# HGRN recurrence: finest level from raw keys, eight mask groups in two PSUM banks, coarse blocks copied by ScalarE, no state work in the last tile

## The chip, the cores and the metric

The kernel runs on one core of a Trainium2 chip. The metric is the device time of one launch in microseconds. Engines are TensorE (PE, with its weight loads PEld), VectorE (DVE), ScalarE (ACT), GpSimd (POOL) and SyncE (SP, here the queue of the weight loads).

## The reference, cut

Two blocks over 512 tokens of width 1024. The first has a gated linear attention (GLA) in chunks of 64 tokens, a short convolution and a window attention; the second runs twice (two layers) and has an indexed attention and the HGRN recurrence. Its intra-chunk part has a decay for each pair of positions and each key channel:

```python
def step(S, xs):
    qc, kc, vc, bc = xs                      # bc = cumsum(log_f) in the chunk
    inter = jnp.einsum('bhtd,bhde->bhte', qc * jnp.exp(bc), S)
    diff = bc[:, :, :, None, :] - bc[:, :, None, :, :]
    decay = jnp.exp(jnp.where(causal[:, :, None], diff, -jnp.inf))
    A = jnp.einsum('bhtd,bhsd,bhtsd->bhts', qc, kc, decay)
    intra = jnp.einsum('bhts,bhse->bhte', A, vc)
    b_last = bc[:, :, -1:, :]
    S = jnp.exp(b_last[:, :, 0, :])[..., None] * S + jnp.einsum(
        'bhsd,bhse->bhde', kc * jnp.exp(b_last - bc), vc)
    return S, inter + intra
```

S after the last chunk is not an output.

## The kernel before, in words

Everything is float32. Projections are products of high and low halves (three matmuls of 512 columns each for one pair of tiles): ScalarE makes the high half of a weight panel (L1029), GpSimd the low half (L1599), SyncE loads panels into a ring of three. Each engine's program is written by hand in its own order and engines meet by semaphores.

The HGRN recurrence (`core`, on TensorE, ScalarE and VectorE) works on tiles of 128 tokens and two heads at a time: eight units per layer, numbered 0 to 7 here, unit u being tile m = u // 2 and heads 2(u % 2), 2(u % 2) + 1. It runs in two layers, from about 983 to 1162 us and from about 1837 to 2015 us of the span. In a unit:

- TensorE sums the logs of the decays with 9 mask groups of 128 columns (7 levels, the running sum, the rest to the tile's end): for each head three banks of 384 columns, L614 and L615. ScalarE takes the exponent of each head's sums (L1171) into `dec`.
- VectorE copies the tile's decay (L1718), then multiplies: rest x keys (L1722), running sum x queries (L1724), and for each of the 7 levels l the odd blocks of width 128 >> (l+1) by queries and the even ones by keys (L1730, 14 operations).
- TensorE turns the rest-keys (L627), computes the diagonal scores (L631) and the scores of the levels (L635, each waits for its `lev_ready`). ScalarE copies the turned keys to `kdt` (L1177). VectorE puts the diagonal (L1734) and the seven levels (L1744) into `attT` by predicated copies from PSUM.
- TensorE makes the unit's output from `attT` and the state (L647, L649), and the state's addend from `kdt` (L653). VectorE copies the output (L1749) and updates the state (L1757).

Between these parts each engine takes steps of other work (`take_on(side, ...)`): projections of the attention's queries, keys and values, 12 matmuls a step. The steps are fixed: one between the sums of the two heads, two after them, one after the levels, one after the output. In units 2 to 5 ScalarE's share of the two steps after the sums is the root of a normalisation: L1212, L1215, L1220, L1222 of 1024 elements each with two table loads (in unit 2 the rectified keys, L1458, too). VectorE's share of the side work is the rotary embedding (L2121, L2127, L2130, L1822, L1824, L2136), the scores of the index (L2047 to L2052) and the selection of the largest (L2059, L2061).

The GLA core (`core_chunked`, from about 108 to 238 us) has the same eight units with two levels and one bank per head.

## Time and profile before

| | |
|---|---|
| time, median of 3 runs | 2625.77 us (2624.51 to 2629.67) |
| profiled execution: span | 2626.2 us |
| its mean granted TensorE clock | 0.994 |
| TensorE busy | 2553.7 us, 97% of the span |
| VectorE busy | 1149.1 us, 44% |
| ScalarE busy | 991.7 us, 38% |
| GpSimd busy | 1082.5 us, 41% |
| chain that ended last | TensorE 80%, VectorE 14%, ScalarE 4%, DMA 1% |

The profiled execution's span is 0.4 us above the median of the three timed runs, so sums made in the trace can be set against the median as they are. A busy share of TensorE counts a matmul from its issue to its modelled end; those ends overlap the next one's start, so prices of matmuls are taken from the distance between starts.

### The profile page before, as it was taken

Reading aid. Unit: us, or ns where it says so; the run is one execution under the profiler, and the core shown is the slowest. Engines: PE = TensorE matmul, PEld = TensorE weight load, DVE = VectorE, ACT = ScalarE, POOL = GpSimd, SP = SyncE. Lnnn points to the kernel's source line nnn. Section 1 sums busy time; section 2 is a strip of 40 time slices with the busy share of each in tenths; the row PEclk is TensorE's granted clock in tenths of the full one; section 3 lists DMA queues with packets and bytes.
Section 4 is the critical chain, followed back from the end, with each engine's and each line's share of the span. In section 5 each row is a group of like instructions: output and inputs, shape, how many; then the busy total and the mean of one; then the engine's idle time right before and its main releaser. Section 6 shows DMA issues by size and latency. Waiting matters only on the chain.

```text
span 2626.2 us, 30117 instructions
## 1 busy us (share of the span) xinstructions
PE 2553.7 (97%) x12440; PEld 2088.4 (80%) x12440; DVE 1149.1 (44%) x1977; ACT 991.7 (38%) x1128; POOL 1082.5 (41%) x816
## 2 busy tenths in 40 slices
PE   7999999999999999989999999999999999999998
PEld 5887777878888787877788888888787778888887
DVE  6452353365424366987434111124698743411112
ACT  4523543343323454635434222235463543422220
POOL 4333334544545443213264444444321326444442
PEclk9999999999999999999999999999999999999999
DMA  4222222322333232222132222233222212222222
GB/s 160 80 79 66 82 80 81 96 97 82 98 99 98 90 97 69 73 64 66 49 96 96 97 96 96 97 97 97 69 73 65 65 50 95 97 97 96 96 96 80
DMA packets 209012, 226.81 MB, mean 86 GB/s; under 512 B 4482, under 2 KB 198236, under 8 KB 208748
## 3 DMA queue, kind: packets, MB, share of 16 engines
q1 hardware_dynamic: 208368, 224.74, 27.0%
q8 instruction: 98, 1.61, 0.3%
q14 instruction: 39, 0.31, 0.0%
q10 hardware_dynamic: 507, 0.15, 0.0%
HBM read 217.01 MB, written 2.10 MB: 83 GB/s over the span
## 4 chain that ended last, share of the span: by engine, by line
PE 80%; DVE 14%; ACT 4%; DMA 1%; issue 1%; SPq 0%; POOL 0%; DVEq 0%; ACTq 0%
PE psum L487 71%; PE psum L764 1%; PE psum L776 1%; PE psum L753 1%; DVE top L2059 1%; DVE attT L1744 1%; ACT wh L1029 1%; DVE ul L1935 1%; PE psum L635 1%; DVE score L2061 1%; DVE dec L1730 1%; DVE normed L1686 1%; DVE merged L1958 1%; DVE tmp L1822 1%; DVE tmp L1824 0%
## 5 line engine op out<-in xcount | busy, mean ns | idle before, releaser
L1599 POOL TENSOR_TENSOR wl<-raw,wh 128x512 fp32r<-128x512 f32 x812 | 1082.3, 1367 | 1519.0 <-ACT wh L1029 1387.3
L487 PE MATMUL psum<-uh,wh 128*128 128x512 f32 x2016 | 803.5, 399 | 13.1 <-DVE ul L1935 4.3
L487 PE MATMUL psum<-uh,wl 128*128 128x512 f32 x2016 | 789.5, 392 | 0.0
L487 PE MATMUL psum<-ul,wh 128*128 128x512 f32 x2016 | 789.0, 391 | 0.0
L1029 ACT CAST wh<-raw 128x2048 fp32r<-128x2048 f32 (+1 forms) x206 | 387.0, 1880 | 299.2 <-DMA raw<-in_w_ffn_out 120.0
L487 PEld LDWEIGHTS psum<-uh,wh 128*128 128x128 f32 x2016 | 380.9, 189 | 101.0 <-issue 13.7
L487 PEld LDWEIGHTS psum<-uh,wl 128*128 128x128 f32 x2016 | 380.5, 189 | 80.7
L487 PEld LDWEIGHTS psum<-ul,wh 128*128 128x128 f32 x2016 | 381.2, 189 | 77.9 <-issue 2.4
L487 PE MATMUL psum<-fh,wl 128*128 128x512 f32 x528 | 205.7, 390 | 0.0
L487 PE MATMUL psum<-fl,wh 128*128 128x512 f32 x528 | 205.7, 390 | 0.0
L487 PE MATMUL psum<-fh,wh 128*128 128x512 f32 x528 | 205.7, 390 | 0.0
L1981 DVE TENSOR_TENSOR xT<-xT,psum 128x1024 f32<-128x1024 f32 (+1 forms) x48 | 56.0, 1166 | 293.0 <-PE psum L487 292.8
L2027 DVE TENSOR_TENSOR tmp<-tmp,psum 128x1024 f32<-128x1024 f32 x22 | 26.9, 1221 | 358.6 <-PE psum L487 358.5
L487 PEld LDWEIGHTS psum<-fl,wh 128*128 128x128 f32 x528 | 99.2, 188 | 20.6
L487 PEld LDWEIGHTS psum<-fh,wl 128*128 128x128 f32 x528 | 99.2, 188 | 20.5
L487 PEld LDWEIGHTS psum<-fh,wh 128*128 128x128 f32 x528 | 99.2, 188 | 20.4
L487 PE MATMUL psum<-vh,wh 128*128 128x512 f32 x280 | 111.4, 398 | 3.0 <-ACT gk L1546 1.4
L487 PE MATMUL psum<-vh,wl 128*128 128x512 f32 x280 | 109.2, 390 | 0.0
L487 PE MATMUL psum<-vl,wh 128*128 128x512 f32 x256 | 99.8, 390 | 0.0
L1389 ACT ACTIVATE tmp<-psum 128x1024 f32<-128x1024 f32 x22 | 22.6, 1029 | 178.5 <-PE psum L487 175.3
L487 PE MATMUL psum<-brh,wh 128*128 128x512 f32 x224 | 89.4, 399 | 0.0
L1171 ACT ACTIVATE dec<-psum 128x1152 f32<-128x1152 f32 x32 | 36.3, 1135 | 139.4 <-PE psum L615 139.4
(353 smaller groups left out, 3343.1 us busy)
## 6 DMA issues: line engine op xcount, KB each, us to landing
raw<-in_w_in SPq DMA_DIRECT2D x78, 1024.0 KB, 5.3
raw<-in_w_ffn_in SPq DMA_DIRECT2D x44, 1024.0 KB, 5.1
raw<-in_w_up SPq DMA_DIRECT2D x22, 1024.0 KB, 5.1
raw<-in_w_ffn_out SPq DMA_DIRECT2D x16, 1024.0 KB, 5.1
raw<-in_w_down SPq DMA_DIRECT2D x8, 1024.0 KB, 5.1
raw<-in_w_out SPq DMA_DIRECT2D x8, 1024.0 KB, 5.1
raw<-in_w_ffn_out SPq DMA_DIRECT2D x8, 768.0 KB, 4.4
raw<-in_w_o SPq DMA_DIRECT2D x4, 1024.0 KB, 5.2
```

What stands on the lines that cost most here:

```text
L487: ins = mm(dst, x, y, start=first and i == 0, stop=last and i == len(todo) - 1)
L635: ins = mm(level_scores(l)[:, i, :, :], dec[:, i, l, :], odd_blocks(dec[:, i, l, :], l), start=True, stop=True)
L753: ins = mm(X[e][:, 0:(b1 - b0) * P], q[HD * e:HD * (e + 1), p, m * P:(m + 1) * P], kof(2 * p + e)[:, b0 * P:b1 * P], start=True, stop=True)
L764: ins = nc.tensor.transpose(X[2][:, c * P:(c + 1) * P], prob[i % 2][:, e, b * P:(b + 1) * P], ident)
L776: ins = mm(X[3][HD * e:HD * (e + 1), 0:P], vof(2 * p + e, b), probT[i % 2][:, e, (b - b0) * P:(b - b0 + 1) * P], start=(b == b0), stop=(b ...
L1029: nc.scalar.copy(wh[p % 3][:, 0:nk * width], raw[p % 3][:, 0:nk * width]).then_inc(S.hi_done, 1)
L1171: fn(dec[:, i, :, :].rearrange("p (b l) t -> p b (l t)", b=3), X4[:, 1:4, 0:3 * P], ACT.Exp).then_inc(S.dec_done, 1)
L1599: ins = nc.gpsimd.tensor_tensor(wl[p % 3][:, w], raw[p % 3][:, w], wh[p % 3][:, w].bitcast(F32), ALU.subtract)
L1686: v.scalar_tensor_tensor(normed[:, c % 2, :], xT[:, c, :], g(c), scale[:], ALU.mult, ALU.mult).then_inc(S.n_normed, 1)
L1730: ins = v.tensor_tensor(e[:, :, :, part, :], e[:, :, :, part, :], x[:, :, :, part, :], ALU.mult)
L1981: v.tensor_tensor(x, x, src, ALU.add).then_inc(pair_free[(n.q - 1) % 2], 1)
L2027: v.tensor_tensor(tmp[2][:], tmp[0][:], src, ALU.mult).then_inc(pair_free[(n.q - 1) % 2], 1)
```

## The change

Three things, in the HGRN core, and the third in the GLA core too.

1. The finest level (blocks of one position) needs no decay on its keys and one step of decay on its queries. It gets no mask group any more: ScalarE takes the exponent of the odd positions' logs out of `lg` into a new tile `last`, VectorE multiplies `last` by the odd queries, and TensorE uses `gk` as it is. Eight mask groups stay, in two banks of 512 columns. The levels' scores move to other columns (l + 2), and the state's addend from X[1] to the second half of X[3]; TensorE waits for the state before a unit's output and not before its sums.
2. The two coarsest levels' blocks are copied from PSUM to `attT` by ScalarE, in three copies behind its `kdt` copy, without a mask. VectorE waits for them (`blocks_done`) before its first predicated copy, and has five levels left.
3. In the last tile (units 6 and 7) nothing is done for the next state: no turned keys, no `kdt`, no addend, no update, no decay copy (none in the first tile either), and no running sum x queries in the first tile.

```diff
 # TensorE, core
-                    if u > 0:
-                        pe.wait_ge(S.state_done, t.up(S.state_done))
...
-                        for b in range(3):
-                            cols = slice(3 * P * b, 3 * P * (b + 1))
-                            mm(X[1 + b][:, 0:3 * P], lth[:, u % 2, i, :], summask[:, cols], start=True, stop=False)
-                            ins = mm(X[1 + b][:, 0:3 * P], ltl[:, u % 2, i, :], summask[:, cols], start=False, stop=True)
+                        for b in range(2):
+                            cols = slice(4 * P * b, 4 * P * (b + 1))
+                            mm(X[1 + b], lth[:, u % 2, i, :], summask[:, cols], start=True, stop=False)
+                            ins = mm(X[1 + b], ltl[:, u % 2, i, :], summask[:, cols], start=False, stop=True)
...
+                            if l + 1 < LEVELS:
+                                keys, queries = dec[:, i, l, :], odd_blocks(dec[:, i, l, :], l)
+                            else:
+                                keys, queries = gk[:, 2 * hp + i, tok], last[:, i, :]
...
+                    if m + 1 < NT:
+                        pe.wait_ge(S.kdt_done, t.up(S.kdt_done))
+                    if 0 < u < CORE_UNITS - 1:
+                        pe.wait_ge(S.state_done, t.up(S.state_done))
 # ScalarE, core
+                        if i == 0:
+                            odd = lg[:, 2 * hp:2 * hp + 2, m * P:(m + 1) * P].rearrange("p h (g two) -> p h g two", two=2)
+                            fn(last[:], odd[:, :, :, 1], ACT.Exp)
...
                     take_on(side, core_steps(total, u, 1))
+                    if m + 1 < NT:
+                        act.wait_ge(S.kd_T, t.up(S.kd_T))
+                        nc.scalar.copy(kdt[:], X[0][:, 0:2 * P].rearrange("p (h f) -> p h f", h=2)).then_inc(S.kdt_done, 1)
+                    act.wait_ge(S.att_done, t.up(S.att_done))
+                    t.up(S.att_done, len(LEVEL_ENDS) - 1)
+                    half, quarter = P // 2, P // 4
+                    nc.scalar.copy(attT[0:half, :, half:P], level_scores(0)[0:half, :, 0, :])
+                    for g in range(2):
+                        keys = slice(half * g, half * g + quarter)
+                        ins = nc.scalar.copy(attT[keys, :, half * g + quarter:half * (g + 1)], level_scores(1)[keys, :, g, :])
+                    ins.then_inc(S.blocks_done, 1)
 # VectorE, core
                     dve.wait_ge(S.att_done, t.up(S.att_done))
+                    dve.wait_ge(S.blocks_done, t.up(S.blocks_done))
...
-                    for l in range(LEVELS):
+                    for l in range(2, LEVELS):
...
 # the levels after which TensorE signals att_done
-LEVEL_ENDS = (1, 3, 6)
+LEVEL_ENDS = (1, 5, 6)
 # the end of core_chunked on TensorE
                 pe.wait_ge(S.out_read, t.up(S.out_read))
-                pe.wait_ge(S.state_done, t.up(S.state_done))
                 finish(side)
```

ScalarE's program in unit 2 of a layer. Before, from the root of the side work to the next unit:

```order
L1222 ACTIVATE tmp<-tmp 128x1024 [waits act_chain]
L1458 ACTIVATE keys_72<-psum 128x1024 [waits pair_full]
L1177 COPY kdt<-psum 128x256 [waits kd_T]
L1029 CAST wh<-raw 128x2048 [waits raw_in1]
L1171 ACTIVATE dec<-psum 128x1152 [waits sums_done]
```

And now:

```order
L1248 ACTIVATE tmp<-tmp 128x1024 [waits act_chain]
L1484 ACTIVATE keys_73<-psum 128x1024 [waits pair_full]
L1193 COPY kdt<-psum 128x256 [waits kd_T]
L1197 COPY attT<-psum 64x2x64 [waits att_done]
L1200 COPY attT<-psum 32x2x32 x2
L1040 CAST wh<-raw 128x2048 [waits raw_in1]
L1185 ACTIVATE last<-lg 128x128 [waits sums_done]
```

The three copies stand behind everything that ScalarE did before `kdt`, and ahead of the next panel's high half. VectorE's program at the same place, before:

```order
L1744 COPY_PREDICATED attT<-pairmask,psum 128x2x64 [waits dve_chain]
L1744 COPY_PREDICATED attT<-pairmask,psum 128x4x32 [waits dve_chain]
L1744 COPY_PREDICATED attT<-pairmask,psum 128x8x16 [waits att_done,dve_chain]
L1744 COPY_PREDICATED attT<-pairmask,psum 128x16x8 [waits dve_chain]
L1744 COPY_PREDICATED attT<-pairmask,psum 128x32x4 [waits att_done,dve_chain]
```

And now, with the sine of the rotary embedding ahead of it:

```order
L2160 SCALAR_TENSOR_TENSOR tmp<-tmp,small,sinT 128x1024 [waits turned]
L1768 COPY_PREDICATED attT<-pairmask,psum 128x256 [waits blocks_done,att_done,dve_chain]
L1778 COPY_PREDICATED attT<-pairmask,psum 128x8x16 [waits att_done,dve_chain]
L1778 COPY_PREDICATED attT<-pairmask,psum 128x16x8 [waits dve_chain]
L1778 COPY_PREDICATED attT<-pairmask,psum 128x32x4 [waits dve_chain]
```

The two coarse copies are gone from VectorE, and its first one waits for ScalarE. On TensorE, at the start of unit 7, before:

```order
L627 MATMUL psum<-const,dec 128x128 [waits out_read,kd_ready,dec_done]
L627 MATMUL psum<-const,dec 128x128
L631 MATMUL psum<-gq,gk 128x128 x2
L635 MATMUL psum<-dec 128x64 [waits lev_ready]
L635 MATMUL psum<-dec 128x64
```

And now:

```order
L633 MATMUL psum<-gq,gk 128x128 [waits out_read,dec_done]
L633 MATMUL psum<-gq,gk 128x128
L641 MATMUL psum<-dec 128x64 [waits lev_ready]
L641 MATMUL psum<-dec 128x64
```

The turned keys are gone there, and with them the wait for VectorE's L1722.

## Rows read from the trace of the kernel before

**Rows 1.** The page: busy time of the engines.
```profile
PE 2553.7 (97%) x12440; PEld 2088.4 (80%) x12440; DVE 1149.1 (44%) x1977; ACT 991.7 (38%) x1128; POOL 1082.5 (41%) x816
```

**Rows 2.** Timeline of TensorE, one head's sums and what follows: start, us.
```profile
1026.35 0.34 PE L614 MATMUL psum<-summask,lth 128*128 128x384 f32 x1
...
1027.41 0.39 PE L487 MATMUL psum<-uh,wh 128*128 128x512 f32 x1
1027.64 0.40 PE L487 MATMUL psum<-ul,wh 128*128 128x512 f32 x1
```

**Rows 3.** Timeline of TensorE, HGRN cores: its idle time in brackets.
```profile
1021.01 1.14 PE L647 MATMUL psum<-attT,gv 128*128 128x128 f32 x4 [1.89 <-DVE attT L1744]
...
1049.02 0.41 PE L614 MATMUL psum<-summask,lth 128*128 128x384 f32 x1 [0.66 <-DVE state L1757]
...
1060.31 0.41 PE L627 MATMUL psum<-const,dec 128*128 128x128 f32 x2 [1.31 <-DVE dec L1722]
...
1067.71 0.49 PE L647 MATMUL psum<-attT,gv 128*128 128x128 f32 x2 [0.61 <-DVE attT L1744]
...
1110.24 0.49 PE L647 MATMUL psum<-attT,gv 128*128 128x128 f32 x2 [0.48 <-DVE attT L1744]
...
1136.28 0.80 PE L647 MATMUL psum<-attT,gv 128*128 128x128 f32 x2 [4.53 <-DVE attT L1744]
...
1153.90 0.41 PE L627 MATMUL psum<-const,dec 128*128 128x128 f32 x2 [0.73 <-issue]
...
1179.32 1.13 PE L806 MATMUL psum<-ik,iq 64*128 64x512 f32 x4 [0.78 <-ACT silu L1227]
...
1913.67 0.41 PE L627 MATMUL psum<-const,dec 128*128 128x128 f32 x2 [1.33 <-DVE dec L1722]
```

**Rows 4.** Windows: busy us of PE, PEld, DVE, ACT, POOL, then granted clock.
```profile
1020.00:1025.00 5.00, 3.99 (x15) 3.52 (x16) 3.20 (x7) 0.00 (x0) 5.00 (x5) 0.66 0.00 0
1910.00:1915.00 5.00, 3.67 (x23) 2.95 (x22) 4.76 (x20) 4.94 (x5) 0.00 (x0) 1.00 0.68 184
```

**Rows 5.** Timeline of ScalarE, units 2, 4 and 5 of the first layer.
```profile
1041.26 0.36 ACT L1177 COPY kdt<-psum 128x256 f32<-128x256 f32 x1
...
1085.90 0.35 ACT L1177 COPY kdt<-psum 128x256 f32<-128x256 f32 x1
...
1106.41 0.35 ACT L1177 COPY kdt<-psum 128x256 f32<-128x256 f32 x1
```

**Rows 6.** Timeline of VectorE, units 2 to 5.
```profile
1039.74 0.45 DVE L1734 COPY_PREDICATED attT<-pairmask,psum 128x256 f32<-128x256 uint8 x1
1040.22 2.63 DVE L1744 COPY_PREDICATED attT<-pairmask,psum 128x128 f32<-128x128 uint8 x7
...
1043.28 3.32 DVE L2049 SCALAR_TENSOR_TENSOR score<-keys,iw,score 128x256 f32<-128x256 f32 x3
...
1085.04 0.45 DVE L1734 COPY_PREDICATED attT<-pairmask,psum 128x256 f32<-128x256 uint8 x1
...
1107.10 0.45 DVE L1734 COPY_PREDICATED attT<-pairmask,psum 128x256 f32<-128x256 uint8 x1
```

**Rows 7.** Timeline of GpSimd, the panel made beside unit 2's side work.
```profile
1043.51 5.52 POOL L1599 TENSOR_TENSOR wl<-raw,wh 128x512 fp32r<-128x512 f32 x4 [16.21 <-ACT wh L1029]
```

**Rows 8.** Timeline of TensorE, then VectorE, the last unit of the GLA core.
```profile
227.66 0.38 PE L692 MATMUL psum<-const,cdec 128*128 128x128 f32 x2
227.88 1.06 PE L697 MATMUL psum<-cdec 128*128 128x128 f32 x8
...
235.15 0.61 PE L713 MATMUL psum<-gv,kdt 128*128 128x128 f32 x4
235.59 0.60 PE L864 MATMUL psum<-const,tmp 128*128 128x128 f32 x4
...
238.39 0.47 PE L487 MATMUL psum<-uh,wh 128*128 128x512 f32 x1 [2.20 <-DVE state L1813]
...
237.69 0.59 DVE L1813 SCALAR_TENSOR_TENSOR state<-state,small,psum 128x128 f32<-128x128 f32 x2
```

More of the change, by code:

```diff
@@ L344, in build_program @@
         csum = at("csum", 38, [P, 4 * P], F32R)
+        last = at("last", 40, [P, 2, P // 2])
         lth = at("lth", 41, [P, 2, 2, P], F32R)
@@ L622, in core @@
                     pe.wait_ge(S.dec_done, t.up(S.dec_done))
-                    pe.wait_ge(S.kd_ready, t.up(S.kd_ready))
                     if u + 1 == CORE_UNITS:
                         pe.wait_ge(S.out_read, t.up(S.out_read))
-                    for i in range(2):
-                        ins = nc.tensor.transpose(X[0][:, i * P:(i + 1) * P], dec[:, i, LEVELS + 1, :], ident)
-                    ins.then_inc(S.kd_T, 1)
+                    if m + 1 < NT:
+                        pe.wait_ge(S.kd_ready, t.up(S.kd_ready))
+                        for i in range(2):
+                            ins = nc.tensor.transpose(X[0][:, i * P:(i + 1) * P], dec[:, i, REST, :], ident)
+                        ins.then_inc(S.kd_T, 1)
                     for i in range(2):
@@ L634, in core @@
                         for i in range(2):
[L635 to L636 removed]
+                            if l + 1 < LEVELS:
+                                keys, queries = dec[:, i, l, :], odd_blocks(dec[:, i, l, :], l)
+                            else:
+                                keys, queries = gk[:, 2 * hp + i, tok], last[:, i, :]
+                            ins = mm(level_scores(l)[:, i, :, :], keys, queries, start=True, stop=True)
                         if l in LEVEL_ENDS:
@@ L648, in core @@
                         if m > 0:
-                            ins = mm(X[0][:, i * P:(i + 1) * P], state[:, h, :], dec[:, i, LEVELS, :], start=False, stop=True)
+                            ins = mm(X[0][:, i * P:(i + 1) * P], state[:, h, :], dec[:, i, CUM, :], start=False, stop=True)
                     ins.then_inc(S.out_done, 1)
-                    for i in range(2):
-                        h = 2 * hp + i
-                        ins = mm(X[1][:, i * P:(i + 1) * P], kdt[:, i, :], gv[:, m, h * P:(h + 1) * P], start=True, stop=True)
-                    ins.then_inc(S.kv_done, 1)
+                    if m + 1 < NT:
+                        for i in range(2):
+                            h = 2 * hp + i
+                            ins = mm(X[3][:, (2 + i) * P:(3 + i) * P], kdt[:, i, :], gv[:, m, h * P:(h + 1) * P],
+                                     start=True, stop=True)
+                        ins.then_inc(S.kv_done, 1)
                     take_on(side, core_steps(total, u, 4))
                 pe.wait_ge(S.out_read, t.up(S.out_read))
-                pe.wait_ge(S.state_done, t.up(S.state_done))
                 finish(side)
@@ L710, in core_chunked @@
                     ins.then_inc(S.out_done, 1)
-                    for i in range(2):
-                        h = 2 * hp + i
-                        ins = mm(X[1][:, i * P:(i + 1) * P], kdt[:, i, :], gv[:, m, h * P:(h + 1) * P], start=True, stop=True)
-                    ins.then_inc(S.kv_done, 1)
+                    if m + 1 < NT:
+                        for i in range(2):
+                            h = 2 * hp + i
+                            ins = mm(X[1][:, i * P:(i + 1) * P], kdt[:, i, :], gv[:, m, h * P:(h + 1) * P], start=True, stop=True)
+                        ins.then_inc(S.kv_done, 1)
                     take_on(side, core_steps(total, u, 4))
                 pe.wait_ge(S.out_read, t.up(S.out_read))
-                pe.wait_ge(S.state_done, t.up(S.state_done))
                 finish(side)
@@ L1727, in core @@
                         form = lambda x: x.rearrange("p h (g two w) -> p h g two w", two=2, w=w)
-                        e, q, k = form(dec[:, :, l, :]), form(gq[:, heads, tok]), form(gk[:, heads, tok])
-                        for part, x in ((1, q), (0, k)):
-                            ins = v.tensor_tensor(e[:, :, :, part, :], e[:, :, :, part, :], x[:, :, :, part, :], ALU.mult)
+                        q, k = form(gq[:, heads, tok]), form(gk[:, heads, tok])
+                        if l + 1 < LEVELS:
+                            e = form(dec[:, :, l, :])
+                            for part, x in ((1, q), (0, k)):
+                                ins = v.tensor_tensor(e[:, :, :, part, :], e[:, :, :, part, :], x[:, :, :, part, :], ALU.mult)
+                        else:
+                            ins = v.tensor_tensor(last[:], last[:], q[:, :, :, 1, 0], ALU.mult)
                         ins.then_inc(S.lev_ready, 1)
@@ L1794, in core_chunked @@
                     scaled(C_KEY, gk).then_inc(S.lev_ready, 1)
-                    scaled(C_CUM, gq)
+                    if m > 0:
+                        scaled(C_CUM, gq)
                     take_on(side, core_steps(total, u, 1))
@@ L2413, in shape_constants @@
         start = (t // w) * w
-        sums.append(np.where(odd, (j >= start) & (j <= t), (j > t) & (j < start + w)))
+        if l + 1 < LEVELS:
+            sums.append(np.where(odd, (j >= start) & (j <= t), (j > t) & (j < start + w)))
         pairs.append(((j // w) % 2 == 0) & (t // w == j // w + 1))
```

104 lines of the change are left out of this document (57 added, 47 removed).

## The prediction

> **What bounds the kernel now.** I read the page first: TensorE is busy 97% of the span [rows 1], so the time falls by what TensorE's own program loses, and by those waits of TensorE that really shrink. Work taken off VectorE or ScalarE counts only there. Next I read TensorE's timeline through the HGRN cores for its idle time. Nearly all of it is VectorE's: L647 waits for the last predicated copy in units 1, 3, 5 and 6, L627 for VectorE's L1722 in units 3 and 7, L614 once for the state [rows 3]. The second layer's core shows the same pattern, so I work out one layer and double it. Then the windows: after the 1.89 us wait the granted clock of a 5 us stretch is 0.66, so it stood at the 1.2 GHz level for two thirds of the stretch and at 2.4 GHz for the rest, and TensorE loses (1 - 0.66) x 5 = 1.7 us; after a wait of 1.33 us (1913.67) the stretch stays at 1.00 [rows 3, 4]. So a wait that grows past something between 1.33 and 1.89 us costs 1.7 us more, and one that shrinks below gives 1.7 back. Last I set the timelines of ScalarE and VectorE beside each other, because the change makes VectorE's first predicated copy wait for ScalarE. In unit 2 VectorE starts it at 1039.74, and ScalarE's kdt copy starts only at 1041.26; in unit 4 it is 1085.04 against 1085.90, in unit 5 1107.10 against 1106.41 [rows 5, 6].
>
> **The change's prices.**
>
> Sums: six matmuls of 384 columns take 1.06 us from start to start, one of 512 takes 0.23, four 0.91: 0.15 saved a head, 0.3 a unit [rows 2]. Matmuls on raw keys in place of scaled ones have the same shapes: nothing.
>
> VectorE: seven predicated copies take 2.63 us [rows 6]; the two that go are of the shorter ones, 0.7 with their gaps. The finest level's second multiplication is 0.2, L1722 and L1724 0.34 each where they go, the decay copy 0.2.
>
> ScalarE: its three copies have 128, 64 and 64 elements a partition, together what one kdt copy has. By elements they cost one kdt copy, 0.36 us; if each costs a whole one, 1.08 [rows 5]. They overlap at their ends as others do; I take 0.4 from kdt's end, near the low end because no element is added, and keep 0.25 to 1.1. By the Trainium skill (ScalarE: Activation LUTs, What ACT_TABLE_LOAD costs: an activation with immediate operands takes 186 ns and 0.833 ns an element, neighbours overlap by 93 ns) the estimate would be 0.5 us behind kdt, which would take some 0.5 us off the gain. The exponent of `last` (128 elements) adds about 0.15 a unit and the smaller `dec` exponents take 0.1 off each.
>
> **One layer, unit by unit** (shift of TensorE, measured from the place where it last waited for nobody or was itself waited for).
>
> Unit 0: sums 0.3, less what the extra exponent adds: -0.25.
> Unit 1: L647 waits on a chain that begins with a DMA of the embedding's halves; its start moves by one head's sums, 0.15, and VectorE saves 0.7: -0.85. TensorE itself arrives 0.3 earlier, so the 1.89 us wait becomes about 1.35, by the row of 1.33 just short of a clock drop.
> Unit 2, head: -0.15.
> Units 2 to 3: the first place where the change hurts. ScalarE is at 1041.5 with its kdt copy (0.1 earlier than before) and at 1041.9 with the blocks, so VectorE starts 2.2 us later than 1039.74, saves 0.7, and is 1.5 us later behind it. It had no slack there: from here to L1722 of unit 3 it never idles. Its three score operations take 3.32 us beside GpSimd's panel of 1043.51 [rows 6, 7], twice their price alone; starting later it meets one more of the panel's pieces, 0 to 0.95 more, I take 0.5. So L1722 of unit 3 is 2.0 later, at 1062.2. TensorE comes there earlier: +0.3 from unit 2's output, -0.66 for the state wait of 1049.02, -0.3 for sums, so its 1.31 us wait becomes 3.9 us and, by rows 3 and 4, the clock falls: 1.8 more. From L627 to L647 is 6.8 us of work (1060.31 to 1067.71 less the 0.61 wait [rows 3]): L647 at 1062.2 + 6.8 + 1.8 = 1070.8 in place of 1067.71: +3.1.
> Unit 4: ScalarE 0.25 earlier, blocks at 1086.4 in place of VectorE's 1085.04; the copies end at 1088.8, TensorE arrives at 1087.9: +0.7.
> Unit 5: blocks and VectorE both at 1106.9; the 0.48 us wait goes: -0.5.
> Unit 6: VectorE alone decides (4.53 us wait): decay 0.2, L1722 0.34, level 0.2, copies 0.7: -1.4. The wait stays above 3 us and the clock drops as before.
> Units 6 to 7: from L647 of unit 6 VectorE loses its state update, 1.0 with the wait ahead of it, the decay copy and L1722, and TensorE loses `kdt`'s turns, L653 and 0.3 of sums; TensorE's 0.73 us wait at 1153.90 moves to the first level, 1.75 earlier: -1.75.
> Tail: the 0.78 us wait of 1179.32 hangs on VectorE's chain behind unit 7's output, from which the 0.6 us state update goes: -0.6.
> Sum: -0.25 - 0.85 - 0.15 + 3.1 + 0.7 - 0.5 - 1.4 - 1.75 - 0.6 = -1.7 a layer, -3.4 for two. Unit 1's clock is worth 1.7 a layer if kept; as my 1.35 lies at the row of 1.33 but with an error of some tenths, I count half: -1.7 for two.
>
> GLA core: unit 6 loses two turns (227.66 to 227.88, 0.22) and L653's like L713 (235.15 to 235.59, 0.45); unit 7 loses 0.2, and at its end TensorE, which waited 2.20 us for the state, now waits for the output's copy only, 0.59 less [rows 8]: -1.45. The wait stays about 2.1, so the clock still drops there.
>
> Sum: -3.4 - 1.7 - 1.45 = -6.5 us; from the median 2625.8, 2619.3.
>
> **Rivals.**
>
> The full gain, 2608 us. ScalarE's copies hold nobody up; then units 2 to 3 give 1.5 and unit 4 0.3, a layer -7.3, in all -14.5 - 1.45 - 1.7 = -17.6. It would need ScalarE to reach its kdt copy before VectorE reaches L1734 in unit 2, 1.5 us earlier than the row shows, and nothing in its program ahead of that place goes. Chance 0.13.
>
> Slower, above 2631 us. The mechanism is the wait for ScalarE's blocks, in units 2 and 4 and, beyond 0.4 us, unit 5. Each us that the three copies take costs 1.0 + 1.0 + 0.6 a layer, 5.2 in two. It cancels the gain at 0.4 + 6.5 / 5.2 = 1.65 us and gives a measurable loss at 2.7 us, 0.9 a copy against 0.36 for kdt. With copies at 1.1 us, one more collision with GpSimd and unit 1 at low clock it is still 2626. The Trainium skill has a rule against this part of the change (ScalarE: Activation LUTs, Rules for kernel authors: plain elementwise work belongs on VectorE, which is faster an element); the time here hangs on when ScalarE is free and not on its speed. Chance 0.12.
>
> My forecast, a gain that ScalarE's lateness eats to a large part, 0.75. Its own range: unit 3 without a clock drop takes 1.9 off each layer and both clocks kept 1.7 in all, 2613; copies at 1.1 us, the collision and no clock kept, 2625.
>
> **Chances and range.** A measurement can tell some 0.2%, 5.2 us, from no change: the bound for faster is 2620.5, just above my number. Of the forecast's 0.75 I give 0.42 to faster, 0.30 to same, 0.03 to slower; with the rivals 0.55, 0.31, 0.14. The range 2609 to 2627 leaves out half of the full gain and nearly all of the slower case.
>
> **What the profile after would show.** Right: four matmuls of 512 columns a head; in unit 2 the first predicated copy starts about 2 us later against ScalarE's chain, released by ScalarE's block copies; TensorE's wait before L627's like in unit 3 near 3.9 us and a clock below 1 behind it; a new wait of about 0.9 us in unit 4; unit 6's wait near 3.4; none for the state before the sums; the unit 1 wait at 1.35. Wrong: no VectorE wait on ScalarE in unit 2, or a unit 3 wait below 2 us (then nearer 2610), or blocks that take over 1 us (then no gain). The number hangs most on unit 3, where VectorE's lateness, GpSimd's panel and the clock multiply each other.

## The result, and the profile after

The changed kernel takes 2630.45 us (median of 20 runs, 2627.35 to 2636.07), the kernel before beside it 2626.76 us (20 runs). The ratio is 1.0017, with a 95% interval of 1.0011 to 1.0022: slower by 4 us. That is less than the 0.2% that I had called measurable, but the interval leaves out 1. I had predicted 2619.3 us, 2609 to 2627.

The profiled execution of the changed kernel spans 2629.6 us (before: 2626.2), so it shows the difference. First the page's row of busy times, the answer to [rows 1]:

```profile
PE 2552.7 (97%) x12340; PEld 2080.0 (79%) x12340; DVE 1128.0 (43%) x1893; ACT 1000.6 (38%) x1186; POOL 1084.4 (41%) x816
```

TensorE has 100 matmuls less and is busy 1.0 us less, VectorE is busy 21 us less: the work did go away. What grew is one stretch of TensorE's program. The timeline of TensorE through the first HGRN core, answering to [rows 3] (the same units in the same order; L655 is L647 of before, L629 is L627):

```profile
1016.35 0.71 PE L655 MATMUL psum<-attT,gv 128*128 128x128 f32 x4 [1.96 <-DVE attT L1778]
...
1039.91 0.49 PE L655 MATMUL psum<-attT,gv 128*128 128x128 f32 x2 [0.38 <-DVE attT L1778]
...
1057.77 0.41 PE L629 MATMUL psum<-const,dec 128*128 128x128 f32 x2 [3.88 <-DVE dec L1750]
...
1058.47 5.17 PE L641 MATMUL psum<-dec 128*128 128x64 f32 x24
1063.43 1.05 PE L641 MATMUL psum<-last,gk 128*128 128x64 f32 x4
...
1069.23 0.38 PE L655 MATMUL psum<-attT,gv 128*128 128x128 f32 x2
...
1090.62 0.49 PE L655 MATMUL psum<-attT,gv 128*128 128x128 f32 x2 [1.02 <-DVE attT L1778]
...
1112.17 0.49 PE L655 MATMUL psum<-attT,gv 128*128 128x128 f32 x2 [0.26 <-DVE attT L1778]
...
1137.51 0.80 PE L655 MATMUL psum<-attT,gv 128*128 128x128 f32 x2 [4.38 <-DVE attT L1778]
```

From one unit's output matmul to the next this gives, after against before:

| stretch, first HGRN layer | before us | after us | difference | predicted |
|---|---|---|---|---|
| unit 0 to 1 | 21.42 | 21.28 | -0.14 | -0.85 |
| unit 1 to 2 | 23.11 | 23.56 | +0.45 | -0.15 |
| unit 2 to 3 | 23.59 | 29.32 | +5.73 | +3.1 |
| unit 3 to 4 | 20.48 | 21.39 | +0.91 | +0.7 |
| unit 4 to 5 | 22.05 | 21.55 | -0.50 | -0.5 |
| unit 5 to 6 | 26.04 | 25.34 | -0.70 | -1.4 |
| unit 6 to 7 | 24.32 | 22.68 | -1.64 | -1.75 |

The second layer has +5.70 in the third row and the others within 0.2 of these, except the last (-0.99). The third row is the result: everything else together is a gain, 1.6 us in the first layer and 1.1 in the second.

In that row two things add. The wait ahead of the turned keys is 3.88 us, as predicted. And behind it TensorE is slow. These are the windows (busy us of PE, PEld, DVE, ACT, POOL, then the granted clock, the DMA share and GB/s) over the wait and what follows:

```profile
1055.00:1060.00 5.00, 2.23 (x14) 2.26 (x15) 4.83 (x21) 4.92 (x6) 0.00 (x0) 0.86 0.02 3
1060.00:1065.00 5.00, 5.00 (x24) 4.90 (x24) 3.40 (x9) 2.46 (x4) 2.17 (x2) 0.50 0.00 0
1065.00:1070.00 5.00, 5.00 (x19) 4.05 (x18) 0.63 (x2) 0.00 (x0) 2.80 (x3) 0.61 0.00 0
```

The granted clock is 0.50 in a whole stretch, the 1.2 GHz level, and it is back at 2.4 GHz only at 1068.7. Summed as (1 - clock) x 5, as the prediction did, that is 0.7 + 2.5 + 1.95 = 5.15 us of clock, where I had put 1.8. TensorE needs 11.46 us from L629 to L655; the same stretch before was 6.8 us of work. At 1063.74 VectorE even waits 1.47 us for TensorE's level matmuls, which it did not in this unit before.

VectorE in unit 2, the answer to [rows 6], and ScalarE and GpSimd beside it, the answer to [rows 5, 7]:

```profile
1037.45 0.46 DVE L1768 COPY_PREDICATED attT<-pairmask,psum 128x256 f32<-128x256 uint8 x1 [2.80 <-ACT attT L1200]
1037.94 1.92 DVE L1778 COPY_PREDICATED attT<-pairmask,psum 128x128 f32<-128x128 uint8 x5
1039.90 0.85 DVE L2086 TENSOR_SCALAR score<-keys,iw 128x256 f32<-128x256 f32 x1
1040.79 4.25 DVE L2088 SCALAR_TENSOR_TENSOR score<-keys,iw,score 128x256 f32<-128x256 f32 x3
1045.07 0.29 DVE L2091 TENSOR_TENSOR score<-score,const 128x128 f32<-128x128 f32 x1
1045.40 0.42 DVE L1783 COPY gq<-psum 128x256 f32<-128x256 f32 x1
...
1057.21 0.42 DVE L1750 TENSOR_TENSOR dec<-dec,gk 128x256 f32<-128x256 f32 x1
```

```profile
1036.50 0.36 ACT L1193 COPY kdt<-psum 128x256 f32<-128x256 f32 x1
1036.75 0.26 ACT L1197 COPY attT<-psum 64x128 f32<-64x128 f32 x1
1036.91 0.41 ACT L1200 COPY attT<-psum 32x64 f32<-32x64 f32 x2
...
1039.33 5.42 POOL L1625 TENSOR_TENSOR wl<-raw,wh 128x512 fp32r<-128x512 f32 x4 [17.24 <-ACT wh L1040]
```

VectorE's first predicated copy waits 2.80 us for ScalarE's blocks, whose three copies end 0.46 us behind the `kdt` copy (1036.86 to 1037.32). The prediction had both, with 2.2 for the wait and 0.4 for the copies.

Where the wait of 3.88 us comes from can be read off, with two rows of before that answer to these. They are VectorE's read of the output (L1749, which is L1783 after) and TensorE's first output matmul of unit 2:

```profile
1047.93 0.42 DVE L1749 COPY gq<-psum 128x256 f32<-128x256 f32 x1
```

```profile
1044.12 0.38 PE L647 MATMUL psum<-attT,gv 128*128 128x128 f32 x2
```

From L1749 to L1722 of unit 3 VectorE took 11.82 us before (TensorE's L627 follows it at 1060.31 [rows 3]), and 11.81 after (1045.40 to 1057.21): it never idles there, so all that matters is when it starts. Before, the last predicated copy of unit 2 ended at 1042.85 [rows 6], 5.08 us ahead of L1749 and 1.27 us ahead of L647. After, it ended at 1039.86, 5.54 us ahead of L1783 and 0.05 ahead of L655. TensorE's own work from L647 to L627 was 14.22 us without its waits, and is 13.98. So VectorE is later against TensorE by 1.22 (it used to be done before TensorE came), 0.46 (more of its score operations beside GpSimd) and 0.24 (TensorE's shorter sums), 1.92 in all. Before, TensorE had waited 0.66 + 1.31 = 1.97 us in two places [rows 3]; after, it waits 1.97 + 1.92 = 3.89 us in one, since the wait for the state no longer stands ahead of the sums.

### The profile page after: what moved, and what is told of

Its sections match the earlier page's. It is cut to its first block, busy times and chain, and to the rows that moved or that the text cites. A ratio compares the mean times of both kernels' runs of the same rounds, so it can differ in the third digit from the quotient of the medians.

```text
span 2629.6 us, 29863 instructions
## 1 busy us (share of the span) xinstructions
PE 2552.7 (97%) x12340; PEld 2080.0 (79%) x12340; DVE 1128.0 (43%) x1893; ACT 1000.6 (38%) x1186; POOL 1084.4 (41%) x816
## 4 chain that ended last, share of the span: by engine, by line
PE 79%; DVE 13%; ACT 6%; issue 1%; DMA 1%; SPq 0%; POOL 0%; DVEq 0%; ACTq 0%
PE psum L490 71%; DVE top L2098 1%; PE psum L775 1%; PE psum L787 1%; PE psum L764 1%; PE psum L641 1%; ACT wh L1040 1%; DVE ul L1974 1%; DVE tmp L2100 1%; DVE attT L1778 1%; DVE score L2100 1%; DVE merged L1997 1%; DVE score L2088 0%; PE psum L895 0%; DVE normed L1712 0%
## 5 line engine op out<-in xcount | busy, mean ns | idle before, releaser
L490 PE MATMUL psum<-brh,wl 128*128 128x512 f32 x224 | 87.4, 390 | 0.0
```

What stands on the lines that cost most here:

```text
L490: ins = mm(dst, x, y, start=first and i == 0, stop=last and i == len(todo) - 1)
```

## The experiments

Each was timed against the kernel before on the same chip (6 to 11 runs each), with ratios and 95% intervals. The median of the kernel before was 2625.9 to 2626.4 us there and 2626.8 beside the change, so a difference between two experiments is good to about a microsecond at best. "Pause" is an idle time of TensorE, in unit 3 where nothing else is said.

**1. VectorE copies all levels.** The rest of the change stays.

```
-                    nc.scalar.copy(attT[0:half, :, half:P], level_scores(0)[0:half, :, 0, :])
...
-                    dve.wait_ge(S.blocks_done, t.up(S.blocks_done))
...
-                    for l in range(2, LEVELS):
+                    for l in range(LEVELS):
```

> The changed kernel with its second part undone: VectorE copies all seven levels, ScalarE none. Theory A (ScalarE's blocks come late in unit 2, VectorE and then TensorE wait, and TensorE's clock falls behind a 3.9 us wait and stays low through the small level matmuls): the wait ahead of unit 3's turned keys goes back to about 1.3 us, the clock stays at 1.00 there, and the time is about 2616 us, some 11 below the kernel before. Rival B (the loss is in the other parts: the extra exponent, the matmuls on raw keys, the state's addend in another bank): the clock or the waits of unit 3 hardly change and the time stays at 2628 or above.

Measured: 2628.52 us, 1.0013 (1.0005 to 1.0022). ScalarE's lateness is then not the whole reason: without any wait for ScalarE the kernel is still slower than before. It is 1.9 us below the change, which these runs don't tell apart. TensorE's timeline and the windows:

```profile
1058.84 0.41 PE L629 MATMUL psum<-const,dec 128*128 128x128 f32 x2 [3.60 <-DVE dec L1743]
```

```profile
1055.00:1060.00 5.00, 1.40 (x10) 1.19 (x8) 4.76 (x19) 4.93 (x5) 0.00 (x0) 0.92 0.21 47
1060.00:1065.00 5.00, 5.00 (x26) 5.00 (x25) 3.89 (x13) 2.86 (x3) 2.07 (x2) 0.50 0.02 3
1065.00:1070.00 5.00, 5.00 (x16) 4.12 (x16) 1.79 (x5) 0.00 (x0) 2.90 (x3) 0.56 0.00 0
```

The pause is 3.60 us and the clock falls as far. VectorE's three score operations take 4.41 us here (3.32 before, where the first of them, begun ahead of GpSimd's panel, takes 0.48 and the two beside it 1.38 each): they fall on another part of the panel, and the collision puts back 1.09 of what ScalarE's absence gives. The removed wait and the shorter sums are in this kernel too.

**2. ScalarE copies only where it is early**, in units 0, 1, 6 and 7; VectorE copies all levels in units 2 to 5.

```
+                    if u in (0, 1, 6, 7):
+                        act.wait_ge(S.att_done, first)
+                        nc.scalar.copy(attT[0:half, :, half:P], level_scores(0)[0:half, :, 0, :])
...
+                    for l in range(2 if u in (0, 1, 6, 7) else 0, LEVELS):
```

> The changed kernel, ScalarE copying the two coarse levels' blocks only in units 0, 1, 6 and 7, where it is free before VectorE comes; VectorE copies them in units 2 to 5. Theory A: as with all copies on VectorE and another 0.7 us a layer in unit 6: about 2614.5 us. Rival B: 2628 or above.

Measured: 2624.87 us, 0.9995 (0.9986 to 1.0004): no difference from the kernel before that can be told, where a gain of some 12 us was expected. The reason is the same: the pause in unit 3 is 3.62 us, and 3.45 us of clock are lost from 1055 to 1065. But it is 5.6 us less than the change and 3.7 less than experiment 1, and the intervals don't meet. ScalarE's copies cost time in units 2 to 5, where they are late, and save time in the other units.

**3. ScalarE's blocks alone**, on the kernel before.

```
+                    nc.scalar.copy(attT[0:half, :, half:P], level_scores(0)[0:half, :, 0, :])
...
+                    dve.wait_ge(S.blocks_done, t.up(S.blocks_done))
...
-                    for l in range(LEVELS):
+                    for l in range(2, LEVELS):
```

> The kernel before with the change's second part alone: ScalarE copies the two coarse levels' blocks in every unit, nothing else. Theory A: units 3 and 4 of each layer lose some 6 us together, the other units gain at most 1: about 2636 us, and the clock is low for some 10 us in unit 3. Rival B: no slower than before, 2620 to 2627.

Measured: 2629.88 us, 1.0016 (1.0007 to 1.0025). A loss of 3.6 us, but far from the 2636 expected. TensorE's waits in units 2 and 3 of the first layer:

```profile
1039.64 0.49 PE L648 MATMUL psum<-attT,gv 128*128 128x128 f32 x2 [0.35 <-DVE attT L1755]
1046.19 0.42 PE L615 MATMUL psum<-summask,lth 128*128 128x384 f32 x1 [2.19 <-DVE state L1768]
1057.48 0.41 PE L628 MATMUL psum<-const,dec 128*128 128x128 f32 x2 [1.30 <-DVE dec L1732]
```

Together 3.49 us, nearly as long as in the changed kernel, but in two pieces, and the windows from 1055 to 1070 show a clock of 1. So the blocks' lateness costs time with the clock up, too. (In the second layer the clock does fall behind the 2.17 us pause, for 1.7 us.) This row gave me the next theory: the pieces matter, not only the sum.

**4. The pause filled.** The changed kernel, with work that nobody reads in unit 3: it adds 16 matmuls of 512 columns. The wait ahead of them keeps the bank that they write free; in the trace of the change that state is done at 1046.34, long ahead of it, so it holds nobody up.

```
+                    if u == 3:
+                        pe.wait_ge(S.state_done, t.at["state_done"] + 1)
+                        for _ in range(16):
+                            mm(X[3], uh[:, 0, 0:P], uh[:, 0, :], start=True, stop=True)
                     pe.wait_ge(S.dec_done, t.up(S.dec_done))
```

> The changed kernel with 16 extra matmuls of 512 columns on idle columns of PSUM in unit 3 of each layer, ahead of the wait for VectorE's turned keys; they take 3.65 us at full clock, a little less than the 3.88 us wait, and do nothing for the result. Theory A: the wait shrinks to about 0.2, nothing comes later for it, the clock stays at 1.00 and each layer gains the 4.7 us that the work behind the wait took too long: about 2621 us. Rival C (the slow stretch behind the wait is not the clock's but the levels' own, held by VectorE's multiplications): no change against the changed kernel, 2630.

Measured: 2621.92 us, 0.9987 (0.9978 to 0.9996). More work, 8.5 us less time. The same three windows:

```profile
1055.00:1060.00 5.00, 4.75 (x34) 4.08 (x33) 4.86 (x21) 4.93 (x8) 0.00 (x0) 1.00 0.01 3
1060.00:1065.00 5.00, 5.00 (x34) 4.44 (x34) 3.56 (x8) 1.91 (x1) 2.99 (x3) 1.00 0.00 0
1065.00:1070.00 5.00, 5.00 (x26) 4.12 (x25) 4.78 (x6) 0.79 (x2) 2.04 (x2) 1.00 0.01 2
```

So the clock in unit 3 is what makes the change a loss. Of the 10.3 us of clock in two layers 8.5 come back.

**5. The wait split again.** Nothing added, one wait moved back to where the kernel before had it.

```
                     pe.wait_ge(S.lt_lo, t.up(S.lt_lo))
+                    if 0 < u < CORE_UNITS - 1:
+                        pe.wait_ge(S.state_done, t.up(S.state_done))
...
-                    if 0 < u < CORE_UNITS - 1:
-                        pe.wait_ge(S.state_done, t.up(S.state_done))
                     for i in range(2):
```

> The kernel after, with one line moved: in the HGRN core TensorE waits for the state's update ahead of the decay sums, as the kernel before did, and no longer ahead of the output matmuls. No work is added or taken away. In the trace of the kernel after, the update in unit 3 of layer 1 ends at 1046.34, and TensorE's sums began at 1044.11 and its wait for the turned keys was 3.88 us: so now about 2.3 us of waiting stand ahead of the sums and 1.6 ahead of the turned keys, 3.9 together as in the kernel after. Theory S (the change joined two waits into one, and the long one lets the clock fall): the granted clock from 1055 to 1070 stays near 1, as in the experiment that filled the wait (2621.9), and the time is 2620 to 2624. Theory T (the sum of waiting decides, however it is split): 2629 to 2632, clock low over the same 11 us or already at the sums.

Measured: 2621.75 us, 0.9985 (0.9976 to 0.9994), 8.7 us less than the change. (One of its 11 runs took 3628.12 us, the others 2620.33 to 2626.66; I have no cause for it.) TensorE's timeline:

```profile
1044.29 0.47 PE L617 MATMUL psum<-summask,lth 128*128 128x512 f32 x1 [2.20 <-DVE state L1792]
...
1063.26 0.49 PE L655 MATMUL psum<-attT,gv 128*128 128x128 f32 x2 [0.87 <-DVE attT L1778]
```

and the windows behind the wait and in unit 3:

```profile
1040.00:1045.00 5.00, 2.80 (x13) 2.00 (x12) 4.83 (x7) 0.00 (x0) 2.56 (x2) 0.97 0.00 0
1045.00:1050.00 5.00, 5.00 (x17) 3.98 (x16) 4.86 (x5) 1.53 (x3) 0.00 (x0) 0.69 0.00 0
...
1055.00:1060.00 5.00, 5.00 (x41) 4.60 (x40) 4.60 (x17) 4.93 (x6) 0.00 (x0) 1.00 0.27 61
1060.00:1065.00 5.00, 4.13 (x25) 3.31 (x24) 2.72 (x8) 2.55 (x5) 2.33 (x2) 1.00 0.00 0
```

The expectation of two pauses was not quite right, and the difference is instructive. The first pause does let the clock fall, by 0.15 + 1.55 = 1.7 us, but these 1.7 us lie ahead of the place where TensorE would have waited 1.6 us more for VectorE. That second pause is gone, so this clock loss is free. A slow stretch costs where TensorE is behind, and nothing where it would wait anyway.

**6. The same, with VectorE copying all levels** (experiment 1 with the wait moved back).

> The same move of the wait in the kernel in which VectorE copies all seven levels (2628.5, its wait in unit 3 3.60 and 3.66 us): parts 1 and 3 of the change, but without the late wait and without ScalarE's blocks. Theory S: the wait splits into about 2.3 and 1.3, no low clock in units 3, and some 3 us a layer less: 2621 to 2624; with the experiment above it says what ScalarE's copies are worth when the clock is out of it. Theory T: 2628 to 2630, as with the late wait.

Measured: 2621.23 us, 0.9983 (0.9974 to 0.9992), 7.3 us less than with the late wait. Against experiment 5 ScalarE's copies make 0.5 us, nothing that can be told. That is a balance and not a price of nothing, as the next experiment shows.

**7. The same, with ScalarE's blocks in units 0, 1, 6 and 7** (experiment 2 with the wait moved back).

> The same move of the wait in the kernel in which ScalarE copies the blocks in units 0, 1, 6 and 7 alone (2624.9, its wait in unit 3 3.62 us with a low clock from 1055 to 1065). Theory S: 2617 to 2620, better than every kernel so far. Theory T: 2624 to 2626.

Measured: 2618.42 us, 0.9974 (0.9962 to 0.9985), 6.5 us less than with the late wait. In all three forms the one moved wait is worth 6 to 9 us. This kernel is also 2.8 us below experiment 6 and 3.3 below experiment 5: with the wait in its place, too, block copies are worth having where ScalarE is early and cost about as much where it is late. (The three intervals overlap, so these two figures are rough.) This trace also holds the same pause twice with two outcomes. Timeline of TensorE and windows, first layer, then second:

```profile
1057.36 0.41 PE L631 MATMUL psum<-const,dec 128*128 128x128 f32 x2 [1.46 <-DVE dec L1752]
1058.06 4.32 PE L643 MATMUL psum<-dec 128*128 128x64 f32 x24
...
1908.34 0.41 PE L631 MATMUL psum<-const,dec 128*128 128x128 f32 x2 [1.45 <-DVE dec L1752]
1909.03 2.85 PE L643 MATMUL psum<-dec 128*128 128x64 f32 x24
```

```profile
1060.00:1065.00 5.00, 5.00 (x21) 4.61 (x21) 4.22 (x10) 2.18 (x3) 2.74 (x3) 0.50 0.00 0
...
1910.00:1915.00 5.00, 5.00 (x33) 4.29 (x32) 4.75 (x14) 3.14 (x4) 1.75 (x2) 1.00 0.00 0
```

A pause of 1.46 us cost 3.4 us of clock, one of 1.45 us in the same place of the other layer none.

**8. The same, with the pauses of units 1 and 6 filled** by work that nobody reads.

```
+                    for _ in range({1: 8, 6: 16}.get(u, 0)):
+                        mm(X[0][:, 0:P], gk[:, 2 * hp, tok], gq[:, 2 * hp, tok], start=True, stop=True)
                     pe.wait_ge(S.pairs_done, t.up(S.pairs_done))
```

> The kernel of the experiment above, and in each HGRN core TensorE also computes 8 matmuls in unit 1 and 16 in unit 6 whose results nobody reads (gk by gq, 128 columns, 0.22 us each, into the first quarter of the bank of the output), ahead of its waits of 1.96 us and 4.4 us for the score blocks. They fill 1.8 and 3.5 us of waiting and none of them is needed. If the clock is what these waits cost beside themselves, the lows at 1015 to 1020, 1130 to 1140, 1905 to 1910 and 1980 to 1990 (granted 0.66, 0.75, 0.91, 0.73, 0.74, 0.91 in that kernel) go, about 1.7 + 1.7 us a layer: 2612 to 2615. If work behind these waits is anyway bound by VectorE, TensorE only waits longer at the next place: 2617 to 2620.

Measured: 2618.16 us, 0.9971 (0.9961 to 0.9981): no gain over experiment 7, although the low clock of unit 6 did go (unit 1 had none left in the trace of experiment 7; the granted clocks in the expectation are those of experiment 2). The edit also takes the wait for `kdt` ahead of the fill. In unit 7 TensorE's wait for VectorE's levels grew from nothing to 1.09 us in the first layer and 1.07 in the second: the second of the two outcomes I had named. Behind unit 6 VectorE sets the time, and TensorE's clock is free there.

**9. Wide work ahead of the narrow.** The changed kernel with its 3.88 us pause; in unit 3 the 12 projection matmuls come directly behind it, ahead of the turns and the level matmuls.

```
                         pe.wait_ge(S.kd_ready, t.up(S.kd_ready))
+                        if u == 3:
+                            take_on(side, core_steps(total, u, 2))
+                            take_on(side, core_steps(total, u, 3))
```

> The kernel after, with the state's wait where it put it; in unit 3 of each HGRN core TensorE takes its 12 matmuls of 512 columns of projection work, which stand behind the level matmuls, right behind its wait for the turned keys instead, ahead of the two turns and of the 28 level matmuls of 64 columns. No work is added and the pause itself (3.88 us) stays. In the kernel after, 6.8 us of work behind that pause took 11.5 us at a granted clock of 0.50 to 0.61. Theory U (what follows the pause decides: behind wide matmuls the clock comes back sooner, behind the narrow level matmuls it stays low): the low stretch costs 1.7 to 3.4 us in place of 5.1, and 2625 to 2628. Theory V (the length of the pause decides, whatever follows): the low stretch costs the same 5.1, now partly under wide matmuls, the level scores come 3 to 5 us later and nothing hides VectorE's copies: 2633 to 2637.

Measured: 2630.44 us, 1.0017 (1.0008 to 1.0026), the time of the changed kernel. TensorE's timeline and the windows:

```profile
1059.03 0.77 PE L490 MATMUL psum<-uh,wh 128*128 128x512 f32 x1 [3.86 <-DVE dec L1754]
...
1063.94 2.79 PE L644 MATMUL psum<-dec 128*128 128x64 f32 x24
...
1068.80 0.75 PE L659 MATMUL psum<-attT,gv 128*128 128x128 f32 x2 [1.62 <-DVE attT L1782]
```

```profile
1060.00:1065.00 5.00, 5.00 (x27) 4.28 (x26) 3.05 (x11) 1.39 (x3) 0.00 (x0) 0.80 0.01 3
1065.00:1070.00 5.00, 3.38 (x26) 3.25 (x26) 2.21 (x6) 2.44 (x4) 2.44 (x2) 0.89 0.00 0
1070.00:1075.00 5.00, 5.00 (x22) 4.34 (x22) 3.60 (x6) 0.00 (x0) 2.51 (x3) 0.77 0.00 2
```

About the clock theory U holds: behind the same pause the low stretch now costs 0.7 + 1.0 = 1.7 us (the window ahead of these, 1055 to 1060, is at 0.86 as in the changed kernel), and the level matmuls run at full speed, 2.79 us in place of 5.17. About the time neither theory holds: nothing covers VectorE's copies any more, so there is a new pause of 1.62 us, and behind it the clock falls again for 1.7 us. What the order of the work saves in one place it gives back in the next.

**10. No state work in the last tile, alone**, on the kernel before.

```
+                    if m + 1 < NT:
+                        pe.wait_ge(S.kd_ready, t.up(S.kd_ready))
+                        for i in range(2):
+                            ins = nc.tensor.transpose(X[0][:, i * P:(i + 1) * P], dec[:, i, LEVELS + 1, :], ident)
```

(and so for `kdt`, L653, the decay and the state, in both recurrences)

> The kernel before with part 3 of the change alone: no state work in the last tile of either recurrence (units 6 and 7), everything else as before (nine mask groups, keys times decay in the finest level, VectorE copies all seven levels, the state's wait ahead of the sums). By the prediction's rows it takes from TensorE two turns (0.41) and four matmuls (0.61) in each of two units of three cores, of which the 4.53 us wait of unit 6 swallows one unit's, and 0.9 to 2.2 us of VectorE's tail at the end of the GLA core: 2622 to 2625. If GLA's end is bound by the transfer or by the output's read, 2625 to 2626.

Measured: 2621.71 us, 0.9979 (0.9970 to 0.9988). This part alone is worth 4.2 us, 0.3 us beyond the good end of the 2622 to 2625 expected. Part 1 (two banks of sums, raw keys) was not run alone; experiment 6 is part 1 and part 3 with the wait in its old place, and differs from this by 0.5 us, so part 1 is worth nothing that can be told. The parts don't simply add: part 2 alone cost 3.6 us, on top of parts 1 and 3 (experiment 5 against 6) 0.5.

**11. Half of the fill** of experiment 4, 8 matmuls.

> The kernel after with 8 matmuls of 512 columns ahead of the wait for the turned keys in unit 3 in place of 16 (1.85 us of unneeded work in a pause of 3.88, so some 2.0 us of pause stay). With 16 the low clock went and the time was 2621.9, with none it is 2630.5. If the clock falls by the length of the one pause, 2.0 us here leave it up (a pause of 2.20 before the sums cost 1.55 us of clock in the split kernel, one of 2.19 none): 2621 to 2624. If any pause ahead of the narrow level matmuls lets it fall (1.46 us did, at 1057.36 in the split kernel with early blocks): 2625 to 2628, a loss of 3.4 us a layer less what later slack takes up.

Measured: 2624.72 us, 1.0000 (0.9990 to 1.0011), between the two answers, and the trace suggests why. The pause is 2.05 us in the first layer and 2.08 in the second:

```profile
1055.00:1060.00 5.00, 3.77 (x19) 3.80 (x19) 4.93 (x19) 4.00 (x8) 0.00 (x0) 0.62 0.01 3
1060.00:1065.00 5.00, 5.00 (x21) 4.71 (x22) 2.48 (x7) 1.88 (x1) 3.05 (x3) 0.50 0.00 0
...
1910.00:1915.00 5.00, 2.92 (x22) 2.41 (x20) 4.79 (x19) 4.93 (x5) 0.00 (x0) 1.00 0.02 3
1915.00:1920.00 5.00, 5.00 (x34) 4.44 (x34) 4.54 (x13) 2.87 (x6) 2.02 (x2) 1.00 0.00 0
```

5.1 us of clock in one layer and nothing in the other. Neither a pause's length nor its place alone decides. Experiment 10 shows the same in unit 1: its pause there is 2.83 us in both layers, and 3.45 us of clock are lost in the first (windows at 0.73 and 0.58 from 1015 to 1025) and none in the second.

**12. Experiment 7 with 6 matmuls of fill** ahead of the 1.46 us pause.

> The kernel with the split wait and ScalarE's blocks in units 0, 1, 6 and 7 (2618.4), and 6 matmuls of 512 columns in unit 3 (1.4 us, results nobody reads) ahead of the wait for the turned keys. In that kernel's trace the wait there was 1.46 us in layer 1 and 1.45 in layer 2; behind the first the granted clock stood at 0.92, 0.50 and 0.90 from 1055 to 1070, a loss of 3.4 us, behind the second it stayed at 1. If this pause costs 3.4 us in some executions and nothing in others, filling it gives half of that twice on the mean, some 2 to 4 us: 2614 to 2617. If not, 2618 to 2619, since the fill takes only idle time.

Measured: 2617.41 us, 0.9970 (0.9959 to 0.9981). The fastest figure, but 1.0 us below experiment 7 is not told apart from it. Experiment 7, which adds no idle work, is the version to keep: 8 us below the kernel before, 12 us below the change.

## Why the prediction was wrong, point by point

What the pauses of unit 3 did to the clock (first layer / second layer; lost is (1 - clock) x 5 summed over the low windows; "state" is ahead of the sums, "keys" ahead of the turned keys and the level matmuls; one traced execution of each kernel):

| kernel | pause us | lost us |
|---|---|---|
| before | keys 1.31 / 1.33 | 0 / 0 |
| 10 | keys 1.33 / 1.33 | 0 / 0 |
| 7 | keys 1.46 / 1.45 | 3.4 / 0 |
| 7 | state 1.92 / 1.91 | 0 / 0 |
| 8 | state 1.92 / 1.93 | 0 / 1.7 |
| 8 | keys 1.44 / none | 0 / - |
| 12 | state 1.91 / 1.95 | 1.7 / 0 |
| 6 | state 1.95 / 2.29 | 1.7 / 1.7 |
| 5 | state 2.20 / 2.19 | 1.7 / 1.7, hidden |
| 3 | state 2.19 / 2.17 | 0 / 1.7 |
| 3 | keys 1.30 / none | 0 / - |
| 11 | keys 2.05 / 2.08 | 5.1 / 0 |
| 2 | keys 3.62 / 3.66 | 3.45 / 3.45 |
| 1 | keys 3.60 / 3.66 | 5.1 / 5.1 |
| after | keys 3.88 / 3.88 | 5.15 / 5.1 |
| 9 | 3.86 / 3.87, wide work behind | 1.7 / 1.7 |
| 9 | ahead of the output 1.62 / 1.63 | 1.7 / 1.7 |

**The step that failed** is in "Units 2 to 3": "so its 1.31 us wait becomes 3.9 us and, by rows 3 and 4, the clock falls: 1.8 more". The mechanism was right and so were the lengths in it: VectorE's lateness 2.0 (measured 2.1: +1.67 from L655 of unit 2 to L629, +0.45 ahead of it), the wait 3.9 (3.88). The size of the clock was wrong: 5.15 us in place of 1.8, of which 4.7 lay on the path. I took 1.7 from [rows 4], a pause that wide matmuls followed, and put it on one that the two turns, four matmuls of 128 columns and 28 of 64 columns follow. Experiment 9 changes only what follows the pause, and there it is 1.7 again. The other traces bear this out in part. Behind the pauses of 3.6 to 3.9 us with the narrow matmuls next, 3.45 us were lost twice and 5.1 four times; behind unit 6's pauses of 3.6 to 5.0 us, where four to eight matmuls of 128 columns and then the projection's of 256 follow, 1.7 us were lost in 15 cases and 3.4 in 11, and never 5.1. So the one row that I read was also the low end of what wide work loses. The miss is 2.6 us a layer, 5.3 in all.

**The cause I gave it was only half of it.** I had the loss grow from ScalarE's late blocks, and my slower rival was slow block copies, which would decide from 1.65 us upward. They took 0.46, and the kernel was slower nevertheless. The late blocks do cost: without them in units 2 to 5 the kernel is 5.6 us faster (experiment 2), and alone they make the kernel before 3.6 us slower (experiment 3). But they don't make the long pause by themselves. Experiments 1 and 2 take them away there and keep pauses of 3.60 and 3.62 us. ScalarE's lateness is 1.22 us of the change's pause, and in experiment 1 GpSimd's collision (1.09) stands in for it. The decisive edit is one that I had in the sum as a shift alone: "-0.66 for the state wait of 1049.02". TensorE did not save these 0.66 us. It carried them, and all other lateness of VectorE, to the next wait, where they make one pause of 3.88 us in place of two. The prediction had that pause right, but did not ask what leaving the wait where it was would save. Moving it back gives 8.7 us.

**Smaller misses.** Unit 1: -0.14 for -0.85. VectorE's 0.7 us was there (from its sine product to the last copy 4.23 us, before 4.94), but the transfer of the embedding's halves let it begin 0.57 us later against the last output (17.00 for 16.43), so the pause stayed 1.96 us. It varies between kernels that issue the same transfer, 0.72 to 2.83 us in this place, and I had moved it by a fixed 0.15; the 1.7 us that I counted for a kept clock did not come. Nor is there a threshold between 1.33 and 1.89 us, as I had read it from two rows. In this unit pauses of 1.96 to 1.99 us were followed by a loss of 1.7 us in the change and by none in experiment 5; in experiments 7 and 9 the clock fell at the start of the first core, behind pauses of 1.3 us that stand 2.5 us apart. Unit 2: +0.45 for -0.15, since the 1.27 us that VectorE was ahead are gone and TensorE now waits 0.38 us; I had looked for this effect only from unit 3 on. Unit 6: -0.70 for -1.4, because GpSimd's panel comes later and one of VectorE's long products meets it (1116.44, 2.20 us for 1.22); that ScalarE's cast behind the block copies is what delays the panel is argued, not shown.

**Right:** unit 4 (+0.91 for +0.7, with the 1.02 us wait), unit 5 (-0.50), the tail (-0.55 for -0.6), the sums (0.13 for 0.15 a head). Units 6 to 7 (-1.64 for -1.75) fit in the first layer alone, and partly by luck: the trace of before lost 3.4 us of clock behind unit 6's pause there and 1.7 in the second layer, where the difference is -0.99. At the end of the GLA core the wait was to change its releaser and the clock to drop still, and this is what the rows show: timeline of TensorE, the answer to [rows 8] (the clock of the window from 235 to 240 is 0.66).

```profile
235.39 0.50 PE L490 MATMUL psum<-uh,wh 128*128 128x512 f32 x1 [2.00 <-DVE gq L1843]
```

That is 3.0 us earlier than before, of which 1.5 stood already at the core's start and came from nothing that the change touches; 1.5 is the predicted 1.45. With the failed step at its measured size, unit 1's clock not kept and units 1, 2 and 6 as measured, the sum is -6.5 + 5.3 + 1.7 + 2 x (0.71 + 0.6 + 0.7) = +4.5 us, against +3.7 measured. That they are so close is in part chance. From unit 0's output to the tail the trace of the change is longer by 3.56 us in the first layer and 4.05 in the second. What brings the whole span back to +3.4 is a lead of 4.5 us at the first layer's unit 0, of which 1.7 were predicted: ahead of that core the trace of before lost 6.85 us of clock and that of the change 3.4, with the same 1.7 at the end of the GLA core in both, so the difference lies where the change does nothing.

The Trainium skill (TensorE: Matmul & The Clock Gate, Why this matters for your kernels) asks to avoid long idle gaps between bursts of matmuls. By it two short waits are better than one of their sum, and the three pairs of experiments with and without the late wait agree (6.5 to 8.7 us). It would have spoken against this change, and I did not weigh it. Another page of the Trainium skill (SBUF — State Buffer, Who interferes with whom) tells that a VectorE instruction with two inputs in SBUF contends with a GpSimd instruction that reads SBUF. The trace agrees in kind: the same three score operations take 3.32, 4.25 and 4.41 us by where GpSimd's panel lies. No run here took GpSimd away.

**What stays open:** why the same pause costs 3.4 or 5.1 us of clock in one layer and nothing in the other (experiments 7 and 11), and with it how much of the difference between narrow and wide work behind a pause is the work itself: experiment 9 has one pause length and one trace. This scatter may also be why a single profile can miss the median by some us: the profiled execution of experiment 6 took 2617.05 us beside a median of 2621.23.

## What to carry to other kernels

A wait that is taken away saves nothing if the engine it waited for is late again at the next wait: add the two, and price the one long pause that results, clock included, ahead of counting the removed one as gain. Price a clock drop by a row in which the same kind of matmul follows the pause. Where the bounding engine must wait for a late one, leave the waits spread out, or put its work between them; and test a sum of many small gains part by part, since here one part (no state work in the last tile) held 4.2 us of gain, block copies were worth having only in the units where ScalarE is early, and one moved line lost 8.7 us.

## What the runs showed of the hardware that I had not expected

Behind a pause of 3.88 us narrow matmuls (28 of 64 columns, 3.2 us at full speed) took 6.0 us and 5.15 us of clock were lost; behind the same pause with wide matmuls first, 1.7 us of clock were lost. Pauses of 1.46 us (once) and 1.62 us (twice) were followed by a low clock, and pauses of 2.08, 2.19 and 2.83 us in other traces or layers were not. All pauses of 3.6 us and more in the HGRN cores were. Three small ScalarE copies out of PSUM (64x128, and two of 32x64) take 0.26 and 0.41 us and end 0.46 us behind the copy ahead of them, so their cost was where they stand and not what they do. Unneeded matmuls in TensorE's idle time made a kernel 8.5 us faster.
